# A feed-forward group taken into the mixer projection's stage, its root multiplied in afterwards

## The chip, the cores and the metric

The kernel runs on one core of one Trainium2 chip. The core's engines each run their own queue of instructions: TensorE (PE for its matmuls, PEld for its weight loads), VectorE (DVE), ScalarE (ACT), GpSimd (POOL) and SyncE (SP), which issues the transfers. The metric is the time of one execution on the device in microseconds (us). Times in brackets of a trace row are idle time of that engine just before the row.

## The reference

The network has two blocks; the change lies in the end of the second block, for 256 tokens of 1024 features. With three mixer branches already computed, that end is:

```
mixed = gates[0] * y_ssm + gates[1] * y_rwkv + gates[2] * y_hgrn
x = x + mixed @ w_out
h_gate, h_up = split(rmsnorm(x, norm2_w) @ ffn_w_in, 2)
x = x + (silu(h_gate) * h_up) @ ffn_w_down
return rmsnorm(x, final_norm_w)

def rmsnorm(x, w): return x * rsqrt(mean(x * x, axis=-1) + eps) * w
```

The factor rsqrt(mean(x*x) + eps) is one number for each token; the text calls it the token's root. A product of the normed x with a matrix is the product of x * w with that matrix, times the token's root.

## The kernel before

Activations lie with features on the 128 partitions and tokens along the row, so x is 8 tiles (`h[:, k, CTX:TOK]`, KT = 8) of 128 x 256 in float32. All weights come as one long stream of chunks of 128 x 1024 numbers (512 KB), four chunks to a group here, into `w_ring`, which has two sets of slots. While one set is multiplied the other is filled. SP issues the loads for the next group when the `used` count says that the group before the present one is done (`Stream.in_stage` inside a stage of mixed work, `Stream.groups` for uniform loops). A matmul of 128 x 128 weights with 256 float32 columns shows in the trace as two matmul records.

The program is a row of stages. Each is a block in which every engine has its own instructions, and at the end of a block all engines meet (line 195). Three stages matter:

- `mixer_out` (lines 3360 to 3426). 32 units of output: 8 for each branch (b = 0, 1, 2) and 8 of `w_out` (b = 3). PE sums a unit into one of six PSUM banks. DVE evacuates it; for b = 3 it adds it to x in `h` (L3419). Then the tail of the norm (`NormTail`) follows: ACT squares the new tile (L3205), DVE adds the squares up in `tail_acc` (L3210), PE sums over the partitions (`column_sums`, L155), DVE makes the mean of it (L3224), POOL raises it to the power of -1/2 (L148), PE spreads the roots over the partitions into bank 7 (`spread`, L162), and DVE writes the eight tiles of x * w * root to `u[:, k, CTX:TOK]` (L3231). Six groups of chunks are taken from the stream.
- `swiglu` (lines 3136 to 3175). 11 groups; in each, PE makes four products of 128 x 256 (two gate tiles, two up tiles) out of eight tiles of `u`, that is 32 matmuls (the helper `accumulate`, L410), into four banks, and the groups take banks 0 to 3 and 4 to 7 in turn. ACT takes the tanh of the gate tiles (L3158), DVE makes silu and multiplies by the up tile (L3166, L3169). `walk` runs the first two groups as written, pairs of groups in a loop, and the last ones as written.
- `residual_norm` multiplies by `ffn_w_down`, adds to x and norms again; it follows `swiglu`.

The stage of `swiglu` is entered by PE only when DVE has written the last tile of `u`, since this is the last thing that is done before the engines meet.

Of the kernel before, what the change touches and what calls it, by code (L numbers as in the profile page):

```python
# [17 lines left out]
ALU = mybir.AluOpType  # L18
# [3 lines left out]
P = 128  # L22
# [3 lines left out]
SEQ = 256  # L26
# [2853 lines left out]
def build(nc, a, out, col_at):  # L2880

    with ExitStack() as top:
        used = {}

        def sb(name, shape, es=top):
            used[name] = used.get(name, 0) + 1
            return es.enter_context(nc.sbuf_tensor(f"{name}_{used[name]}", shape, F32))
# [19 lines left out]
        def tail_work(n, es2):  # L2907
            return [sb("tail_" + name, [P] + d, es2) for name, d in (("sq", [2, n]), ("acc", [n]), ("rs", [TT]))]
# [189 lines left out]

        yh = sb("yh", [P, HG, SEQ])
        gates = sb("gates", [P, 24, SEQ])  # L3100
        with ExitStack() as es:
            with ExitStack() as e3:
                work = [sb("hg_" + n, [P] + d, e3) for n, d in (
                    ("e", [2, 512]), ("qx", [2, SEQ]), ("kx", [2, SEQ]), ("sm", [2, SEQ]), ("ib", [2, ST, P]), ("osq", [SEQ]),
                    ("rc", [2, ST]), ("sd", [SEQ]), ("kd", [SEQ]), ("pairs", [LEVELS * P]), ("gt", [HG, SEQ]))]
                hgrn_heads(nc, st, bank, banks, C2, cs, p_hg, lf, kf, cc("hgrn_norm_w"), yh, work, latent, gates[:, 8:24, :], 16, 4)

        with ExitStack() as es:

            mixer_out(nc, st, bank, C, (ys, yr, yh), early, gates, h, hold, late, tail_work(SEQ, es), u, cc("norm2_w"))  # L3110
            nc.sync.sem_clear(late)

        with ExitStack() as es:
            ffn = sb("ffn", [P, FF, SEQ], es)
            ffn_tanh = sb("ffn_tanh", [P, 2, 2, SEQ], es)
            swiglu(nc, st, bank, latent, ffn, ffn_tanh)
# [19 lines left out]
def swiglu(nc, st, bank, src, out, th):  # L3136

    count = FF // 2
    st.begin(4)
    with stage(nc, "used tanh doubled done") as (s, block):  # L3140
        def tensor(pe):
            def visit(g, h, r):
                if not isinstance(g, int) or g >= 2:
                    pe.wait_ge(s["done"], g * 2 - 2)
                for m in range(4):
                    st.wait(pe, h, r, m)
                    mm = accumulate(nc, bank[4 * h + m][:, 0:SEQ], [st.chunk(h, m)[:, P * k:P * k + P] for k in range(KT)],
                                    [src(k) for k in range(KT)])
                mm.then_inc(s["used"], 1)
            walk(pe, count, visit)  # L3150

        def scalar(act):
            def visit(g, h, r):
                act.wait_ge(s["used"], g + 1)
                if not isinstance(g, int) or g >= 2:
                    act.wait_ge(s["done"], g * 2 - 2)
                for m in range(2):
                    nc.scalar.activation(th[:, h, m, :], bank[4 * h + m][:, 0:SEQ], ACT.Tanh, scale=0.5).then_inc(s["tanh"], 1)  # L3158
            walk(act, count, visit)

        def vector(dve):
            def visit(g, h, r):
                for m in range(2):

                    dve.wait_ge(s["tanh"], g * 2 + 2)
                    nc.vector.scalar_tensor_tensor(th[:, h, m, :], th[:, h, m, :], 1.0, bank[4 * h + m][:, 0:SEQ],  # L3166
                                                   ALU.add, ALU.mult).then_inc(s["doubled"], 1)
                    dve.wait_ge(s["doubled"], g * 2 + (m + 1))
                    nc.vector.scalar_tensor_tensor(out[:, bass.ds(g * 2 + m, 1), :].rearrange("p a t -> p (a t)"), th[:, h, m, :], 0.5,  # L3169
                                                   bank[4 * h + 2 + m][:, 0:SEQ], ALU.mult, ALU.mult).then_inc(s["done"], 1)  # L3170
            walk(dve, count, visit)
            dve.wait_ge(s["done"], 2 * count)
# [184 lines left out]
    st.passed(groups, per_body)  # L3357


def mixer_out(nc, st, bank, C, branches, early, gates, h, hold, reloaded, work, u, g_cols):  # L3360
# [8 lines left out]
    with stage(nc, "used mixed " + NormTail.NAMES) as (s, block):  # L3369
# [36 lines left out]
        def _(dve):  # L3406
            link = Chain(dve, s["dve_own"])
            for q, (b, m) in enumerate(units):
                ps, mixed = bank[q % banks][:, 0:SEQ], gates[:, m, :]
# [12 lines left out]
            tail.add(dve, link, KT - 1)  # L3422
            tail.mean(dve, link)
            tail.scale(dve, link, u, g_cols)

    st.passed(6, 4)


def fm(w, cols=None):
# [117 lines left out]
```

## Time and profile before

| what | value |
|---|---|
| median of 3 runs | 2105.58 us (2104.49 to 2110.91) |
| the profiled execution's own time | 2105.29 us |
| its span in the trace | 2103.3 us |
| PE busy in matmuls | 1937.8 us, 92% |
| DVE, ACT, POOL busy | 1019.4, 601.8, 75.3 us |
| mean granted TensorE clock | 0.965 of full |
| stream of weights and other transfers | 184.73 MB, mean 88 GB/s |

A granted clock of 1.00 is 2.4 GHz, 0.50 is 1.2 GHz. The end of a matmul record is modelled; records overlap, so the distance between starts, and not the duration, says how fast they follow each other. The trace's own time runs from the first instruction to the last (the span); the execution takes 1.99 us more.

### The profile page before, as it was taken

What the parts mean: (1) busy time and instruction counts of PE and PEld (TensorE: products, weight loads), DVE (VectorE), ACT (ScalarE), POOL (GpSimd) and SP (SyncE); (2) the same over time, 40 slices, a digit from 0 to 9 for tenths busy, and PEclk for the clock granted to TensorE, in tenths of its full rate; (3) what the DMA queues carried; (4) which work ended last, traced back from release to release, by engine and by line L of the source; (5) the groups of instructions that cost most, each with busy time, mean ns of one, the idle gap of its engine ahead of it and who ended that gap; (6) DMA issues with size and microseconds to landing.
All of it is one profiled execution on the core that took longest, in us unless ns stands there. A gap on an engine that the chain in (4) does not pass through costs nothing. (4 is left out here: it accounts for less than half of the span.)

```text
span 2103.3 us, 40179 instructions
## 1 busy us (share of the span) xinstructions
PE 1937.8 (92%) x16700; PEld 1425.0 (68%) x16700; DVE 1019.4 (48%) x2050; ACT 601.8 (29%) x1287; POOL 75.3 (4%) x51
## 2 busy tenths in 40 slices
PE   6989999999999998798998799989889899989998
PEld 2566666666666766343575687767775898878886
DVE  3456676757676766212125458774545542311001
ACT  2234344434344444201014143233332321000000
POOL 0001010101010110000000000010000000000000
PEclk9999999999999999899999899989999999999999
DMA  9021212111011010222220432231002222433343
GB/s 379 18 82 51 102 41 102 51 62 41 32 32 41 22 41 22 80 80 80 86 80 30 148 136 80 102 112 61 32 33 111 81 80 81 178 112 145 144 180 140
DMA packets 52240, 184.73 MB, mean 88 GB/s; under 512 B 5856, under 2 KB 9312, under 8 KB 51552
## 3 DMA queue, kind: packets, MB, share of 16 engines
q1 hardware_dynamic: 52064, 182.23, 23.7%
q8 instruction: 130, 2.13, 0.4%
q14 instruction: 46, 0.38, 0.1%
HBM read 180.11 MB, written 2.10 MB: 87 GB/s over the span
## 5 line engine op out<-in xcount | busy, mean ns | idle before, releaser
L843 PE MATMUL banks<-u,w_ring 128*128 128x512 f32 x768 | 362.5, 604 | 2.0 <-DVE u L680 2.0
L386 PE MATMUL banks<-u,w_ring 128*128 128x256 f32 x1056 | 251.9, 391 | 8.4 <-PEq L195 8.4
L386 PEld LDWEIGHTS banks<-u,w_ring 128*128 128x128 f32 x1056 | 200.3, 196 | 42.4 <-issue 17.1
L843 PEld LDWEIGHTS banks<-u,w_ring 128*128 128x128 f32 x768 | 139.5, 193 | 124.9 <-issue 117.5
L410 PE MATMUL banks<-u,w_ring 128*128 128x256 f32 x704 | 155.0, 384 | 4.8 <-PEq L195 4.8
L410 PEld LDWEIGHTS banks<-u,w_ring 128*128 128x128 f32 x704 | 135.6, 193 | 24.0 <-issue 5.0
L3316 PE MATMUL banks<-gated,w_ring 128*128 128x512 f32 (+1 forms) x384 | 140.7, 529 | 2.9 <-PEq L195 2.9
L3316 PEld LDWEIGHTS banks<-gated,w_ring 128*128 128x128 f32 x384 | 73.8, 193 | 69.3 <-issue 66.0
L871 DVE SCALAR_TENSOR_TENSOR acc<-raw,hc,acc 128x512 f32<-128x512 f32 x128 | 96.2, 752 | 4.6
L3316 PE MATMUL banks<-ffn,w_ring 128*128 128x256 f32 x352 | 77.9, 385 | 3.0 <-PEq L195 3.0
L3316 PEld LDWEIGHTS banks<-ffn,w_ring 128*128 128x128 f32 x352 | 68.0, 193 | 12.9 <-issue 3.3
L3166 DVE SCALAR_TENSOR_TENSOR ffn_tanh<-ffn_tanh,banks 128x256 f32<-128x256 f32 x22 | 9.2, 418 | 137.9 <-ACT ffn_tanh L3158 137.9
L1269 ACT ACTIVATE acc<-banks 128x512 f32<-128x512 f32 x80 | 47.8, 597 | 83.6 <-PE banks L1092 82.1
L1360 DVE TENSOR_TENSOR acc<-acc,banks 128x512 f32<-128x512 f32 x80 | 55.0, 688 | 32.5 <-PE banks L1108 30.2
L1356 DVE TENSOR_TENSOR y<-banks,const_base 128x512 f32<-128x512 f32 x80 | 55.3, 692 | 28.5 <-PE banks L1080 26.7
L3205 ACT ACTIVATE tail_sq<-h 128x256 f32<-128x256 f32 (+1 forms) x28 | 13.2, 471 | 194.6 <-DVE h L2950 91.7
L1108 PEld LDWEIGHTS banks<-y,acc 64*64 64x64 f32 x2560 | 45.8, 134 | 28.9 <-DVE y L1356 21.8
L1296 ACT ACTIVATE dec<-banks,hs 128x128 f32<-128x128 f32 x128 | 47.0, 367 | 56.9 <-PE banks L1203 53.8
L1381 DVE SCALAR_TENSOR_TENSOR rn<-banks,hs,v_t 128x128 f32<-128x128 f32 x96 | 33.7, 351 | 56.9 <-PE banks L1193 54.3
L1213 PEld LDWEIGHTS banks<-dec,h 128*128 128x128 f32 x256 | 35.7, 197 | 37.1 <-ACT dec L1300 27.1
L1108 PE MATMUL banks<-y,acc 64*64 64x64 f32 x2560 | 55.4, 222 | 3.5 <-DVE y L1356 2.5
L2950 DVE SCALAR_TENSOR_TENSOR h<-banks,mod,h 128x256 f32<-128x256 f32 x16 | 7.7, 484 | 101.8 <-PE banks L3316 101.5
(498 smaller groups left out, 3198.0 us busy)
## 6 DMA issues: line engine op xcount, KB each, us to landing
w_ring<-in_w SPq DMA_DIRECT2D x289, 512.0 KB, 5.6
gated<-in_ada SPq DMA_DIRECT2D x32, 512.0 KB, 4.3
h<-in_h SPq DMA_DIRECT2D x2, 2048.0 KB, 9.6
const_base<-in_const SPq DMA_DIRECT2D x1, 1216.0 KB, 5.3
hold<-h SPq DMA_DIRECT2D x1, 1024.0 KB, 5.2
const_part<-in_const SPq DMA_DIRECT2D x1, 1024.0 KB, 4.7
h<-hold SPq DMA_DIRECT2D x1, 1024.0 KB, 10.2
out<-u SPq DMA_DIRECT2D x8, 128.0 KB, 1.9
```

The source lines that it names most:

```text
L386: mm = self.nc.tensor.matmul(place, self.st.chunk(g % 2, slot)[:, P * k:P * k + P], self.src(k), start=(k == 0), stop=(k == KT - 1))
L410: last = nc.tensor.matmul(out, lhs[k], rhs[k], start=(k == 0), stop=(k == n - 1))
L843: mm = nc.tensor.matmul(self.places[m % len(self.places)][:, :], (st.slot(m) if g is None else st.chunk(g % 2, m))[:, P * k:P * k + P], u[ ...
L871: link(nc.vector.scalar_tensor_tensor(out, raw[:, m, :, i:i + SEQ], hc[:, 5 * m + i:5 * m + i + 1], out, ALU.mult, ALU.add), self.s["conv" ...
L1108: mm = nc.tensor.matmul(block_of(bank[2 * d + j], t, hb), invt_c[half(j), d, 2 * t + hb, :], prod[half(j), d, hb, t, :], start=True, stop= ...
L1213: mm = nc.tensor.matmul(tile(bank[3 + d], j), tile(qkd[:, 2 * j + d, :], t), tile(vn[:, d, :], j), start=True, stop=True)
L1269: link(nc.scalar.activation(invt_c[:, d].rearrange("p s e -> p (s e)"), bank[4 + d][:, :], ACT.Copy), s["t_out"])
L1296: link(nc.scalar.activation(tile(vn[:, d, :], j), tile(bank[2], 2 * d + j), ACT.Copy, scale=col(BETA, 2 * j + d, t)), s["vn_ready"] if j a ...
L1356: link(nc.vector.tensor_tensor(prod[:, d], both(sums(2 * d, 256)), mask(d, lv), ALU.mult), s["p_ready"])
L1360: link(nc.vector.tensor_tensor(by_chain(inv[:, d]), by_chain(inv[:, d]), both(sums(2 * d, 256)), ALU.subtract), s["t_ready"])
L1381: link(nc.vector.scalar_tensor_tensor(tile(resid[:, d, :], j), tile(bank[0], 2 * d + j), col(NEG_EG, 2 * j + d, t), v_t[:, t, j, :], ALU.m ...
L3316: mm = nc.tensor.matmul(bank[m % banks][:, 0:n], st.chunk(g % 2, c)[:, P * (at % 8):P * (at % 8) + P], src(k), start=(k == 0), stop=(k == ...
```

## The change

The first of the 11 feed-forward groups moves from `swiglu` into the end of `mixer_out`, which now takes seven groups from the stream. It is summed from x * w without the root. For this ACT writes x * w to the free half of `u` (`u[:, k, 0:SEQ]`) as soon as a tile of x is there, ahead of its square. PE does the group's four products (`rough`) around the tail's own two steps. The units' banks are turned by four places, so that the products can go to banks 0 to 3. ACT copies the spread roots from bank 7 to a new tile `root` in SBUF, and DVE's eight scaling instructions read them there. In `swiglu` DVE first multiplies the four banks by `root` and goes on with silu; ten groups are left for the loop, and they start with the other half of the banks.

```diff
 def swiglu(nc, st, bank, src, out, th, root):
-    count = FF // 2
+    count = FF // 2 - 1
...
-                if not isinstance(g, int) or g >= 2:
-                    pe.wait_ge(s["done"], g * 2 - 2)
+                if not isinstance(g, int) or g >= 1:
+                    pe.wait_ge(s["done"], g * 2)
...
-                    mm = accumulate(nc, bank[4 * h + m][:, 0:SEQ], [st.chunk(h, m)[:, P * k:P * k + P] for k in range(KT)],
+                    mm = accumulate(nc, bank[4 - 4 * h + m][:, 0:SEQ], [st.chunk(h, m)[:, P * k:P * k + P] for k in range(KT)],
...
         def scalar(act):
+            for m in range(2):
+                act.wait_ge(s["rooted"], 2 * m + 2)
+                nc.scalar.activation(out[:, m, :], th[:, 0, m, :], ACT.Tanh, scale=0.5).then_inc(s["rough_tanh"], 1)
...
         def vector(dve):
+            for m in range(2):
+                for up in range(2):
+                    nc.vector.tensor_tensor(th[:, up, m, :], bank[2 * up + m][:, 0:SEQ], root, ALU.mult).then_inc(s["rooted"], 1)
+            for m in range(2):
+                dve.wait_ge(s["rooted"], 2 * m + 2)
+                dve.wait_ge(s["rough_tanh"], m + 1)
+                nc.vector.scalar_tensor_tensor(out[:, m, :], out[:, m, :], 1.0, th[:, 0, m, :], ALU.add, ALU.mult).then_inc(s["doubled"], 1)
+                dve.wait_ge(s["doubled"], m + 1)
+                nc.vector.scalar_tensor_tensor(out[:, m, :], out[:, m, :], 0.5, th[:, 1, m, :], ALU.mult, ALU.mult).then_inc(s["done"], 1)
...
-    through = [0, 4, 8, 16, 24, 28, 32]
+    place = lambda q: (q + 4) % banks
+    through = [0, 4, 8, 16, 24, 28, 32, 33]
...
-        st.in_stage(6, 4, s["used"], block, through, {3: reload})
+        st.in_stage(7, 4, s["used"], block, through, {3: reload})
...
-                    mm = nc.tensor.matmul(bank[q % banks][:, 0:SEQ], st.chunk(g % 2, c)[:, P * at:P * at + P],
+                    mm = nc.tensor.matmul(bank[place(q)][:, 0:SEQ], st.chunk(g % 2, c)[:, P * at:P * at + P],
...
-            tail.sums(pe)
+            def rough(c):
+                st.wait(pe, 6 % 2, 6 // 2, c)
+                pe.wait_ge(s["evacuated"], len(units) - banks + c + 1)
+                for k in range(KT):
+                    if c == 0:
+                        pe.wait_ge(s["primed"], k + 1)
+                    mm = nc.tensor.matmul(bank[c][:, 0:SEQ], st.chunk(6 % 2, c)[:, P * k:P * k + P], u[:, k, 0:SEQ],
+                                          start=(k == 0), stop=(k == KT - 1))
+                return mm
+            rough(0)
+            pe.wait_ge(s["added"], KT - 1)
+            column_sums(nc, C, bank[7], tail.acc, tail.tiles).then_inc(s["sums"], 1)
+            rough(1)
+            pe.wait_ge(s["root"], 1)
+            spread(nc, C, bank[7], tail.rs, tail.tiles).then_inc(s["spread"], 1)
+            rough(2)
+            rough(3).then_inc(s["used"], 1)
...
             for k in range(KT):
+                act.wait_ge(s["evacuated"], 3 * KT + k + 1)
+                link(nc.scalar.activation(u[:, k, 0:SEQ], tail.tile(k), ACT.Copy, scale=g_cols[:, k:k + 1]), s["primed"])
                 tail.square(act, link, k)
+            act.wait_ge(s["spread"], 1)
+            link(nc.scalar.activation(root, bank[7][:, 0:SEQ], ACT.Copy), s["copied"])
...
             tail.mean(dve, link)
-            tail.scale(dve, link, u, g_cols)
+            dve.wait_ge(s["copied"], 1)
+            tail.scale(dve, link, u, g_cols, root)
```

On PE, at the end of `mixer_out`, the program reads as follows; L3394 is the units' matmul of before and L3409 the same line after, L3420 is the matmul of `rough`, L155 the column sums, L162 the spread, L195 the meeting of the engines. Counts are matmuls.

```order
-L3394 MATMUL banks<-gates,w_ring 128x256 x64
+L3396 UNCONDITIONAL_BRANCH
+L3409 MATMUL banks<-u,w_ring 128x256 x64
+L3409 MATMUL banks<-yr,w_ring 128x256 x32
+L3409 MATMUL banks<-yh,w_ring 128x256 x32
+L3409 MATMUL banks<-gates,w_ring 128x256 x64
+L3420 MATMUL banks<-u,w_ring 128x256 x8
 L155 MATMUL banks<-const_base,tail_acc 128x1 x2
+L3420 MATMUL banks<-u,w_ring 128x256 x8
 L162 MATMUL banks<-const_base,tail_rs 128x128 x2
+L3420 MATMUL banks<-u,w_ring 128x256 x16
 L195 UNCONDITIONAL_BRANCH
```

Before, the column sums came straight behind the units and the spread straight behind the sums; now 8 matmuls stand ahead of each of the two and 16 behind the spread.

On ACT, at the end of `mixer_out` and the start of `swiglu`; L3205 is the square of before and L3219 the same after, L3438 writes x * w, L3441 copies the roots, L3156 is the tanh of the moved group and L3158 (after: L3162) that of the others.

```order
+L3438 ACTIVATE u<-h,cols 128x256
+L3219 ACTIVATE tail_sq<-h 128x256
+L3441 ACTIVATE root<-banks 128x256
 L195 UNCONDITIONAL_BRANCH
 L288 UNCONDITIONAL_BRANCH
-L3158 ACTIVATE ffn_tanh<-banks 128x256 x4
+L3156 ACTIVATE ffn<-ffn_tanh 128x256 x2
+L3162 ACTIVATE ffn_tanh<-banks 128x256 x4
```

Each of the eight squares now has one more instruction of ACT ahead of it, and one copy stands behind the last square.

On SP, around the reload of a spilled tile inside `mixer_out` (L3374 before, L3389 after); L215 is the load of one chunk, L304 the clearing of the ring's counts ahead of the stage's last group of loads.

```order
 L215 DMA w_ring<-in_w 128x1024 x16
-L3374 DMA h<-hold 128x8x256
-L215 DMA w_ring<-in_w 128x1024 x4
+L3389 DMA h<-hold 128x8x256
+L215 DMA w_ring<-in_w 128x1024 x8
 L304 ISA
 L215 DMA w_ring<-in_w 128x1024 x4
```

Four chunk loads have moved from the stage of `swiglu` into this one, behind the reload.

## Rows read from the trace of the kernel before

**Rows 1.** The page, its parts 1 and 5: busy time by engine; costliest groups by line.

```profile
PE 1937.8 (92%) x16700; PEld 1425.0 (68%) x16700; DVE 1019.4 (48%) x2050; ACT 601.8 (29%) x1287; POOL 75.3 (4%) x51
...
L410 PE MATMUL banks<-u,w_ring 128*128 128x256 f32 x704 | 155.0, 384 | 4.8 <-PEq L195 4.8
```

**Rows 2.** The timeline of the mixer projection's end: start us, duration us, engine, line.

```profile
1844.80 2.75 PE L3394 MATMUL banks<-gates,w_ring 128*128 128x256 f32 x12
...
1847.66 0.42 DVE L3419 SCALAR_TENSOR_TENSOR h<-banks,h 128x256 f32<-128x256 f32 x1 [2.57 <-PE banks L3394]
1848.12 0.99 DVE L3210 TENSOR_TENSOR tail_acc<-tail_acc,tail_sq 128x256 f32<-128x256 f32 x2
1848.17 0.42 ACT L3205 ACTIVATE tail_sq<-h 128x256 f32<-128x256 f32 x1 [3.04 <-DVE h L3419]
...
1849.17 0.61 PE L155 MATMUL banks<-const_base,tail_acc 128*128 128x1 f32 x4 [1.61 <-DVE tail_acc L3210]
1849.88 0.16 DVE L3224 TENSOR_SCALAR tail_rs<-banks 128x2 f32<-128x2 f32 x1 [0.77 <-PE banks L155]
1850.12 0.69 POOL L148 TENSOR_TENSOR tail_rs<-tail_rs,const_base 128x2 f32<-128x2 f32 x1 [89.79 <-DVE tail_rs L3224]
...
1850.87 0.43 PE L162 MATMUL banks<-const_base,tail_rs 128*128 128x128 f32 x2 [1.10 <-POOL tail_rs L148]
1851.42 4.10 DVE L3231 SCALAR_TENSOR_TENSOR u<-h,cols,banks 128x256 f32<-128x256 f32 x8 [1.38 <-PE banks L162]
...
1856.11 24.18 PE L410 MATMUL banks<-u,w_ring 128*128 128x256 f32 x98 [4.81 <-PEq L195]
1856.21 18.53 SPq L215 DMA_DIRECT2D w_ring<-in_w  x8
1872.99 0.66 ACT L3158 ACTIVATE ffn_tanh<-banks 128x256 f32<-128x256 f32 x2 [24.41 <-PE banks L410]
```

**Rows 3.** Busy time and granted clock of PE by stretches: start:end, length, busy, PEclk.

```profile
1848.00:1851.00 3.00, 0.73 (x5) 1.00 0.00 0
1851.50:1856.00 4.50, 0.00 (x0) 0.50 0.00 0
1857.00:1861.00 4.00, 4.00 (x11) 0.50 0.79 294
1862.50:1866.50 4.00, 4.00 (x20) 1.00 0.25 100
1900.00:1950.00 50.00, 50.00 (x233) 1.00 0.45 168
1462.00:1465.00 3.00, 1.85 (x31) 1.00 0.00 0
...
2015.50:2018.50 3.00, 3.00 (x9) 0.50 0.90 345
```

**Rows 4.** The timeline of ACT in the feed-forward groups, second and last.

```profile
1886.81 0.66 ACT L3158 ACTIVATE ffn_tanh<-banks 128x256 f32<-128x256 f32 x2 [13.16 <-PE banks L410]
...
2011.13 0.66 ACT L3158 ACTIVATE ffn_tanh<-banks 128x256 f32<-128x256 f32 x2 [13.07 <-PE banks L410]
```

**Rows 5.** The timeline of PE at 1089 us, a spread that waits for nothing.

```profile
1089.15 0.60 PE L162 MATMUL banks<-const_base,att_rq 128*128 128x128 f32 x4
1089.59 3.60 PE L1518 MATMUL banks<-kf,pqz 128*128 128x512 f32 x8
```

**Rows 6.** The boundary between two stages at 1370 us, by line L195.

```profile
L195 PEldq EVENT_SEMAPHORE  x2: 51/51/51, 1369.3 to 1370.1; - x2
...
L195 ACTq EVENT_SEMAPHORE  x2: 17/17/17, 1369.9 to 1370.1; - x2
```

**Rows 7.** The timeline of PE at 1370 us, behind that boundary.

```profile
1370.18 1.10 PE L386 MATMUL banks<-u,w_ring 128*128 128x256 f32 x4 [0.99 <-PEq L195]
```

**Rows 8.** The timeline of PE at 1464 us, behind another boundary.

```profile
1463.90 1.97 PE L2235 MATMUL banks<-const_part,lw_rw 128*128 128x256 f32 x8 [1.15 <-PEq L195]
```

**Rows 9.** The timeline of PE behind the feed-forward groups.

```profile
2014.05 6.24 PE L3316 MATMUL banks<-ffn,w_ring 128*128 128x256 f32 x20 [2.96 <-PEq L195]
```

**Rows 10.** DMA from 1825 to 1880 us in 40 slices of 1.375 us.

```profile
DMA  9400000898930000000000059688100000039898
GB/s 366 197 6 0 0 0 0 259 405 313 399 149 0 12 0 0 0 0 0 0 0 0 0 176 393 244 304 331 77 0 0 0 0 0 0 92 381 331 355 331
```

**Rows 11.** What the DMA queue itself waited for, 1760 to 2103 us.

```profile
SPq L215 <- PE banks L410: 107.5, 9, 15.0
```

More of the change, by code:

```diff
@@ L3100, in build @@
         gates = sb("gates", [P, 24, SEQ])
+        root = sb("root", [P, SEQ])
         with ExitStack() as es:
@@ L3108, in build @@
         with ExitStack() as es:
-            mixer_out(nc, st, bank, C, (ys, yr, yh), early, gates, h, hold, late, tail_work(SEQ, es), u, cc("norm2_w"))
+            mixer_out(nc, st, bank, C, (ys, yr, yh), early, gates, h, hold, late, tail_work(SEQ, es), u, cc("norm2_w"), root[:, :])
             nc.sync.sem_clear(late)
@@ L3115, in build @@
             ffn_tanh = sb("ffn_tanh", [P, 2, 2, SEQ], es)
-            swiglu(nc, st, bank, latent, ffn, ffn_tanh)
+            swiglu(nc, st, bank, latent, ffn, ffn_tanh, root[:, :])
             def add(m, ps, link, done):
@@ L3133, in build, with swiglu @@
         st.drain()
-def swiglu(nc, st, bank, src, out, th):
-    count = FF // 2
+def swiglu(nc, st, bank, src, out, th, root):
+    count = FF // 2 - 1
     st.begin(4)
-    with stage(nc, "used tanh doubled done") as (s, block):
+    with stage(nc, "rooted rough_tanh used tanh doubled done") as (s, block):
         def tensor(pe):
             def visit(g, h, r):
-                if not isinstance(g, int) or g >= 2:
-                    pe.wait_ge(s["done"], g * 2 - 2)
+                if not isinstance(g, int) or g >= 1:
+                    pe.wait_ge(s["done"], g * 2)
                 for m in range(4):
                     st.wait(pe, h, r, m)
-                    mm = accumulate(nc, bank[4 * h + m][:, 0:SEQ], [st.chunk(h, m)[:, P * k:P * k + P] for k in range(KT)],
+                    mm = accumulate(nc, bank[4 - 4 * h + m][:, 0:SEQ], [st.chunk(h, m)[:, P * k:P * k + P] for k in range(KT)],
                                     [src(k) for k in range(KT)])
@@ L3152, in scalar @@
         def scalar(act):
+            for m in range(2):
+                act.wait_ge(s["rooted"], 2 * m + 2)
+                nc.scalar.activation(out[:, m, :], th[:, 0, m, :], ACT.Tanh, scale=0.5).then_inc(s["rough_tanh"], 1)
             def visit(g, h, r):
                 act.wait_ge(s["used"], g + 1)
-                if not isinstance(g, int) or g >= 2:
-                    act.wait_ge(s["done"], g * 2 - 2)
+                act.wait_ge(s["done"], max(g * 2, 2) if isinstance(g, int) else g * 2)
                 for m in range(2):
-                    nc.scalar.activation(th[:, h, m, :], bank[4 * h + m][:, 0:SEQ], ACT.Tanh, scale=0.5).then_inc(s["tanh"], 1)
+                    nc.scalar.activation(th[:, 1 - h, m, :], bank[4 - 4 * h + m][:, 0:SEQ], ACT.Tanh, scale=0.5).then_inc(s["tanh"], 1)
             walk(act, count, visit)
         def vector(dve):
+            for m in range(2):
[7 more added lines that the diff above has]
+                nc.vector.scalar_tensor_tensor(out[:, m, :], out[:, m, :], 0.5, th[:, 1, m, :], ALU.mult, ALU.mult).then_inc(s["done"], 1)
             def visit(g, h, r):
@@ L3165, in visit @@
                     dve.wait_ge(s["tanh"], g * 2 + 2)
-                    nc.vector.scalar_tensor_tensor(th[:, h, m, :], th[:, h, m, :], 1.0, bank[4 * h + m][:, 0:SEQ],
+                    nc.vector.scalar_tensor_tensor(th[:, 1 - h, m, :], th[:, 1 - h, m, :], 1.0, bank[4 - 4 * h + m][:, 0:SEQ],
                                                    ALU.add, ALU.mult).then_inc(s["doubled"], 1)
-                    dve.wait_ge(s["doubled"], g * 2 + (m + 1))
-                    nc.vector.scalar_tensor_tensor(out[:, bass.ds(g * 2 + m, 1), :].rearrange("p a t -> p (a t)"), th[:, h, m, :], 0.5,
-                                                   bank[4 * h + 2 + m][:, 0:SEQ], ALU.mult, ALU.mult).then_inc(s["done"], 1)
+                    dve.wait_ge(s["doubled"], g * 2 + (m + 3))
+                    nc.vector.scalar_tensor_tensor(out[:, bass.ds(g * 2 + (2 + m), 1), :].rearrange("p a t -> p (a t)"), th[:, 1 - h, m, :],
+                                                   0.5, bank[6 - 4 * h + m][:, 0:SEQ], ALU.mult, ALU.mult).then_inc(s["done"], 1)
             walk(dve, count, visit)
-            dve.wait_ge(s["done"], 2 * count)
+            dve.wait_ge(s["done"], 2 * count + 2)
         st.groups(count, 4, s, block, ((block.tensor, tensor), (block.scalar, scalar), (block.vector, vector)))
@@ L3357, in residual_norm, with mixer_out @@
     st.passed(groups, per_body)
-def mixer_out(nc, st, bank, C, branches, early, gates, h, hold, reloaded, work, u, g_cols):
+def mixer_out(nc, st, bank, C, branches, early, gates, h, hold, reloaded, work, u, g_cols, root):
     banks = 6
     units = [(b, m) for b in range(4) for m in range(KT)]
-    through = [0, 4, 8, 16, 24, 28, 32]
+    place = lambda q: (q + 4) % banks
+    through = [0, 4, 8, 16, 24, 28, 32, 33]
     st.begin(4)
-    with stage(nc, "used mixed " + NormTail.NAMES) as (s, block):
+    with stage(nc, "used mixed primed copied " + NormTail.NAMES) as (s, block):
         tail = NormTail(nc, C, s, bank[7], h, CTX, SEQ, work, 3 * KT)
@@ L3408, in _ @@
             for q, (b, m) in enumerate(units):
-                ps, mixed = bank[q % banks][:, 0:SEQ], gates[:, m, :]
+                ps, mixed = bank[place(q)][:, 0:SEQ], gates[:, m, :]
                 own = gates[:, 8 * b + m, :] if b < 3 else None
@@ L3423, in _ @@
             tail.mean(dve, link)
-            tail.scale(dve, link, u, g_cols)
-    st.passed(6, 4)
+            dve.wait_ge(s["copied"], 1)
+            tail.scale(dve, link, u, g_cols, root)
+    st.passed(7, 4)
 def fm(w, cols=None):
```

## The prediction, made before the changed kernel ran

> **What bounds the kernel now.** I read the page first: PE is busy for 92% of the span, every other engine for less than half [rows 1]. So what counts is where PE stands still or runs slowly near the change, and the next view is the timeline of the place where one stage hands over to the other [rows 2]. The reader is to follow one chain there. The last record of the mixer's matmuls ends at 1844.80 + 2.75 = 1847.55. DVE then takes the tile (1847.66), ACT squares it (1848.17), DVE adds, PE sums at 1849.17, DVE and POOL make the root (done at 1850.81), PE spreads it from 1850.87, and DVE writes eight scaled tiles from 1851.42, for 4.10 us. Only then can the engines meet, and the first feed-forward matmul starts at 1856.11. From 1847.55 to there are 8.56 us, in which PE's own work is 0.61 + 0.43 us.
>
> The granted clock, read next by stretches [rows 3], shows a second loss. It is 1.00 (2.4 GHz) when PE falls silent, 0.50 (1.2 GHz) from 1851.5 on, still 0.50 between 1857 and 1861 with PE busy throughout, and 1.00 from 1862.5. So group 0 of the feed-forward runs its first records at half speed.
>
> What that costs comes from ACT, whose tanh marks the end of each group. Groups 1 and 10 end at 1886.81 and 2011.13 [rows 4], nine groups apart: 124.32 / 9 = 13.81 us a group. A group is 704 / 11 = 64 records [rows 1], so 0.216 us each, in agreement with 233 records in 50 us at full clock, some records being lost [rows 3]. Group 0 took 1872.99 - 1856.11 = 16.88 us [rows 2]. At full clock it would take 13.81 plus about 0.3 us (the first weight load uncovered, the last record running out, ACT's start), my estimate from the same rows: a record lasts longer than the 0.216 between starts. So 14.1 us, and 2.8 us are lost to the clock.
>
> **The change part by part.** All times are against the profiled execution.
>
> PE, what goes. The idle stretch of 8.56 us is filled by a group that had to be done anyway: -8.56. The group now follows the units without a pause, and its start at half clock goes: -2.8.
>
> PE, what stays as work. Column sums and spread now stand between products. The trace has a spread that waits for nothing, between long matmuls: four records take 1089.59 - 1089.15 = 0.44 us, 0.11 each [rows 5]. Here it is four records for the sums and two for the spread [rows 2]: 6 x 0.11 = 0.66. The upper bound is their stand-alone time, 0.61 + 0.43 = 1.04. I take +0.66, since they are ready when PE comes to them, as in rows 5. The products and these end at 1847.55 + 13.81 + 0.66 = 1862.0.
>
> PE, the new boundary. Before, PE waited there for DVE; now PE is last. At 1370 us PE reached the meeting at 1369.3 and ACT at 1369.9, and PE's pause was 0.99 us [rows 6, 7]; another boundary has 1.15 [rows 8]. In both a slower engine came after PE. In the first, 0.3 us pass from the last arrival to PE's next matmul, and PE and SP need some 0.15 to arrive. So the bounds are 0.45 and 1.15, and I take +0.6, near the lower one because nothing is expected behind PE. Group 1 then starts at 1862.6 and ends at 1876.7, against 1886.81.
>
> What must be ready for PE, with its slack. (a) Product 0, step 7 needs the last x * w. DVE's tile is there at 1848.08, ACT's new instruction, 0.42 like the square beside it [rows 2], ends at about 1848.6, and PE asks at 1847.55 + 7 x 0.43 = 1850.6: slack 2. (b) The squares are now behind that instruction: last square to 1849.1, last add (0.5) to 1849.6, PE asks for the sums at 1847.55 + 3.45 = 1851.0: slack 1.4. (c) Sums done at 1851.4; the root came 1.03 us after them before (1849.78 to 1850.81), so at 1852.5, and PE wants it at 1854.9: slack 2.4. (d) ACT copies the roots at about 1855.2 (two tanh from PSUM take 0.66, so 0.33), DVE scales for 4.1 us to 1859.8, and its arrival at the meeting has 2.2 us in hand. Reading the roots from SBUF has no row of its own; the instruction that reads a bank beside SBUF takes 0.42 at L3419 and 0.51 here [rows 2], so 3.4 to 4.1 in all, and both fit. Each of these costs nothing while its slack holds, and one for one beyond it.
>
> The stream. The moved group's chunks were already loaded in this stage: the DMA share falls to zero after slice 11 from 1834.6, that is by 1841.5 [rows 10], 6 us before `rough` asks. The next group is now issued when the units end, at 1847.6, instead of at 1856.21 [rows 2]; the same load took until about 1864.9 then (slices 23 to 28), 9 us, so it lands at about 1856 for a use at 1862.6. The reload of the tile sits ahead of both in SP's queue as before. SP waited for PE 107.5 us in nine waits in the feed-forward loop, not PE for SP [rows 11].
>
> DVE and ACT in `swiglu`. The moved group is finished behind PE's group 1: four multiplications, two tanh, four steps of silu, ten instructions of at most 0.5 us, some 4 us with their waits, from 1862.5. PE asks for those banks only at the next group, at 1876.7, and ACT has nothing else till then. The waits of the later groups keep their distance of two groups.
>
> Sum: -8.56 - 2.8 + 0.66 + 0.6 = -10.1 us. All later stages only move up. 2105.29 - 10.1 = 2095.2 in the profiled execution; the median of before lies 0.29 above it, so 2095.5.
>
> **The rivals.**
>
> *The clock still falls.* PE's stream is now interrupted three times within 15 us: sums, spread, boundary. If one of them lets the clock fall as it did at 1851.5, PE runs at half speed for the length of that fall, some 10 us [rows 3], and loses 5: gain 5.1, time 2100.4. For it: the pause of 2.96 us behind the feed-forward [rows 9] is followed by a stretch at 0.50 [rows 3]. Against: around the 1.15 us pause of rows 8 the clock stays 1.00 [rows 3], and each interruption here is shorter.
>
> The Trainium skill ("TensorE: Matmul & The Clock Gate", section "A second HAM failure mode: psum-queue depth-cycling") speaks for this rival: short idle gaps between groups of matmuls, as they move from bank to bank, were seen to make the clock swing and to cost throughput. By that rule the time would be the 2100.4 just given; the feed-forward loop of this trace, which changes banks all the time at 1.00, does not bear it out, and I leave it little.
>
> *The tail chain is late.* If one of (a) to (d) is over its slack, PE stands there. What is wanted for a loss is more than 1.4 us of unseen latency in a chain of 2 us; the price is then 1 or 2 us, 2096.5 to 2097.5. It stays inside my range.
>
> *The stream is the bound.* Then PE's head start is given back as a wait for chunks before the next groups, and the time is 2105.5. Against it: PE is busy 50.00 of 50.00 us in the loop while the DMA share is 0.45 [rows 3], and up to 405 GB/s against 168 were moved [rows 10].
>
> *Slower.* The low clock stays: from the sums on PE is never again busy enough, and works at 1.2 GHz until the feed-forward loop is well under way. Half clock costs half of its length, so it breaks even at 20 us and shows as slower beyond 33 us. If it lasted from 1851 to the end of group 2, 42 us, it would cost 21 and give 2116.5. In this trace half clock ended some 6 us after PE was busy again [rows 2, 3], which is strongly against it.
>
> *The change doesn't do what it says.* The order on PE shows 32 matmuls ahead of the boundary and 32 fewer behind, so only unexpected waits could undo it.
>
> **How the numbers follow.** Forecast 0.80; late tail 0.04; clock falls 0.10; stream 0.03; slower 0.03. The likeliest is 2095.5. One fall of the clock behind the pause of rows 9 costs about 1.5 us (3 us at half [rows 3]) and may come or not in a given run, and the boundary adds 0.15 or takes 0.55. That gives 2093.3 to 2098; towards the rival at 2100.4 I go on to 2101, and 2092.8 below. A difference under 0.3%, 6.3 us, is not told from none. Forecast, a short fall of the clock and late tail are faster: 0.85. The full fall and the stream are within 0.3%: 0.12. Slower: 0.03.
>
> **What would show it.** In the profile after: L3420 starts within 0.3 us of the end of the units; sums and spread in 0.11 us a record with no pause before either; PEclk 1.00 from 1848 to past 1865; a pause of PE of 0.5 to 1.2 us at the boundary, DVE there first by about 2 us; the tanh of the first group that `swiglu` sums at about 1876.7, the other nine 13.81 us apart, and the end of the last ten us earlier. The forecast is wrong if PE pauses before L155 or L162, if a stretch at 0.50 lies in the first group of `swiglu`, or if the loop's groups become longer.

## The result, and the profile after

The changed kernel is faster: 2092.18 us median of 5 runs (2091.18 to 2094.99), against 2105.46 us (2101.63 to 2110.91) of the kernel before, a ratio of 0.9937 (95% interval 0.9919 to 0.9955), that is 13.3 us. The forecast was 2095.5 us in a range from 2092.8 to 2101.0. Direction and mechanism were right; the time lies 0.6 us below the range. In two further sets of runs (e2 and e8 below) the ratio was 0.9949 and 0.9948, 10.7 and 10.9 us.

The place of the change, in the timeline of the kernel after (start us, duration us, engine, line; L3409 is the units' matmul, L3420 the moved group's, L3457 the evacuation, L3438 x * w, L3219 the square):

```profile
1839.80 4.48 PE L3409 MATMUL banks<-gates,w_ring 128*128 128x256 f32 x20
...
1844.11 3.62 PE L3420 MATMUL banks<-u,w_ring 128*128 128x256 f32 x16
...
1844.38 0.42 DVE L3457 SCALAR_TENSOR_TENSOR h<-banks,h 128x256 f32<-128x256 f32 x1 [2.57 <-PE banks L3409]
...
1844.90 0.51 ACT L3438 ACTIVATE u<-h,cols 128x256 f32<-128x256 f32 x1 [2.50 <-DVE h L3457]
...
1845.96 0.42 DVE L3224 TENSOR_TENSOR tail_acc<-tail_acc,tail_sq 128x256 f32<-128x256 f32 x1 [0.70 <-ACT tail_sq L3219]
...
1847.57 0.50 PE L155 MATMUL banks<-const_base,tail_acc 128*128 128x1 f32 x4
...
1848.41 0.69 POOL L148 TENSOR_TENSOR tail_rs<-tail_rs,const_base 128x2 f32<-128x2 f32 x1 [91.08 <-DVE tail_rs L3238]
...
1851.46 0.38 PE L162 MATMUL banks<-const_base,tail_rs 128*128 128x128 f32 x2
...
1851.94 0.38 ACT L3441 ACTIVATE root<-banks 128x256 f32<-128x256 f32 x1 [6.08 <-PE banks L162]
1852.47 4.13 DVE L3245 SCALAR_TENSOR_TENSOR u<-h,cols,root 128x256 f32<-128x256 f32 x8 [4.13 <-ACT root L3441]
...
1859.21 23.12 PE L410 MATMUL banks<-u,w_ring 128*128 128x256 f32 x106 [0.45 <-PEq L195]
...
1873.30 0.66 ACT L3162 ACTIVATE ffn_tanh<-banks 128x256 f32<-128x256 f32 x2 [12.22 <-PE banks L410]
```

Against [rows 2] the reader is to see four things. The first `rough` matmul starts at 1844.11, before the modelled end of the units' last record (1839.80 + 4.48 = 1844.28). The column sums (L155) and the spread (L162) have no idle time before them. DVE scales from 1852.47 to 1856.60, while PE works to 1858.75, so the last eight instructions that [rows 2] had in front of the feed-forward cost nothing. And the pause of PE at the boundary is 0.45 us instead of 4.81. The granted clock of the same stretches (length, busy, PEclk):

```profile
1844.00:1848.00 4.00, 4.00 (x23) 1.00 0.64 236
1848.00:1852.00 4.00, 4.00 (x21) 1.00 0.74 289
1852.00:1859.00 7.00, 6.75 (x32) 1.00 0.00 0
1859.00:1863.00 4.00, 3.79 (x18) 1.00 0.69 244
...
2002.00:2005.00 3.00, 3.00 (x9) 0.50 0.96 335
```

It is 1.00 from the units through the whole first group of `swiglu`, where [rows 3] had 0.50 from 1851.5 to past 1861. The stretch at 0.50 behind the feed-forward loop is still there. ACT's second and last tanh of the loop's ten groups:

```profile
1887.11 0.66 ACT L3162 ACTIVATE ffn_tanh<-banks 128x256 f32<-128x256 f32 x2 [13.16 <-PE banks L410]
...
1997.62 0.66 ACT L3162 ACTIVATE ffn_tanh<-banks 128x256 f32<-128x256 f32 x2 [13.15 <-PE banks L410]
```

(1997.62 - 1887.11) / 8 = 13.81 us a group, as in [rows 4].

Where the whole difference lies is told by four stretches: all stages ahead of the mixer projection, that stage, `swiglu`, and what follows. First before, then after (start:end, length, busy, PEclk):

```profile
0.00:1762.72 1762.72, 1618.04 (x15249) 0.97 0.21 76
1762.72:1856.11 93.39, 85.87 (x390) 0.96 0.40 147
1856.11:2014.05 157.94, 154.98 (x704) 0.98 0.39 146
2014.05:2103.30 89.25, 78.94 (x358) 0.95 0.44 165
```

```profile
0.00:1759.47 1759.47, 1612.70 (x15248) 0.97 0.21 76
1759.47:1859.21 99.74, 99.29 (x455) 0.98 0.42 158
1859.21:2000.54 141.33, 138.37 (x640) 1.00 0.40 149
2000.54:2089.40 88.86, 78.94 (x358) 0.95 0.44 166
```

From the first matmul of the mixer projection to the first one behind the loop it is 2014.05 - 1762.72 = 251.33 us before and 2000.54 - 1759.47 = 241.07 after: 10.26 less. Behind that, 0.39 less. But the first stretch, with the same program, is shorter too: 3.25. Together 13.9 of span, and 0.2 outside it (about 2.0 us of the execution lie outside the span before, 1.8 after). The profiled execution of the changed kernel, 2091.18 us, is also the fastest of its five. The text below calls the 251.33 and 241.07 the *distance*.

### The profile page after: what moved, and what is told of

It is laid out like the page before. It is cut to its first block and busy times, and to the rows that moved or that the text cites. A ratio compares the mean times of both kernels' runs of the same rounds, so it can differ in the third digit from the quotient of the medians.

```text
span 2089.4 us, 40176 instructions
## 1 busy us (share of the span) xinstructions
PE 1929.3 (92%) x16700; PEld 1418.8 (68%) x16700; DVE 1020.4 (49%) x2054; ACT 606.4 (29%) x1296; POOL 75.3 (4%) x51
## 5 line engine op out<-in xcount | busy, mean ns | idle before, releaser
L386 PE MATMUL banks<-u,w_ring 128*128 128x256 f32 x1056 | 249.7, 388 | 8.4 <-PEq L195 8.4
L386 PEld LDWEIGHTS banks<-u,w_ring 128*128 128x128 f32 x1056 | 198.8, 194 | 41.7 <-issue 17.1
L843 PEld LDWEIGHTS banks<-u,w_ring 128*128 128x128 f32 x768 | 139.5, 193 | 125.0 <-issue 117.7
L410 PE MATMUL banks<-u,w_ring 128*128 128x256 f32 x640 | 138.4, 379 | 0.5 <-PEq L195 0.5
L410 PEld LDWEIGHTS banks<-u,w_ring 128*128 128x128 f32 x640 | 121.5, 190 | 17.3 <-issue 0.8
L3219 ACT ACTIVATE tail_sq<-h 128x256 f32<-128x256 f32 (+1 forms) x28 | 13.2, 470 | 173.5 <-DVE h L2950 91.7
```

Source lines behind the costliest of these rows:

```text
L386: mm = self.nc.tensor.matmul(place, self.st.chunk(g % 2, slot)[:, P * k:P * k + P], self.src(k), start=(k == 0), stop=(k == KT - 1))
L410: last = nc.tensor.matmul(out, lhs[k], rhs[k], start=(k == 0), stop=(k == n - 1))
L843: mm = nc.tensor.matmul(self.places[m % len(self.places)][:, :], (st.slot(m) if g is None else st.chunk(g % 2, m))[:, P * k:P * k + P], u[ ...
```

## The experiments

Ten runs. Each measured gain comes from the ratio to the kernel before, timed beside it; a 95% interval stands behind it. The changed kernel's own gain by distance is 10.25 us, and a variant's profile says how much of that it keeps. The table gives, for each profile, where the mixer projection starts, the distance, and the length from there to the end.

| kernel | start of mixer projection | distance | to the end | ratio (95%) |
|---|---|---|---|---|
| before | 1762.72 | 251.33 | 89.22 | |
| after | 1759.47 | 241.07 | 88.82 | 0.9937 (0.9919 to 0.9955) |
| e1 before again | 1761.28 | 251.34 | 89.21 | 1.0000 (0.9991 to 1.0009) |
| e2 after again | 1761.00 | 241.10 | 88.83 | 0.9949 (0.9936 to 0.9963) |
| e8 after, third time | 1763.62 | 241.07 | 88.82 | 0.9948 (0.9934 to 0.9962) |
| e7 places only | 1766.87 | 251.34 | 89.22 | 0.9999 (0.9990 to 1.0009) |
| e3 keep busy | 1763.55 | 248.54 | 89.22 | 0.9989 (0.9979 to 0.9999) |
| e4 root first | 1760.77 | 246.42 | 88.52 | 0.9966 (0.9954 to 0.9978) |
| e5 root last | 1764.12 | 248.89 | 88.83 | 0.9992 (0.9982 to 1.0002) |
| e9 spread late | 1764.32 | 244.23 | 87.15 | 0.9972 (0.9961 to 0.9983) |
| e6 early tanh, on after | 1769.48 | 239.47 | 87.14 | 0.9928 (0.9914 to 0.9941) |
| e10 early tanh alone | 1761.28 | 249.73 | 87.14 | 0.9979 (0.9970 to 0.9988) |

### e1, e2, e7, e8: are the 3 us ahead of the change its own?

Two theories. A: they are scatter of the unchanged stages, and the change is worth 10.6. B: the change's layout (a new tile, turned banks, other addresses) makes the stages ahead faster.

e1 is the kernel before with no edit.

> The kernel before, unchanged, once more. In the profiles the way from the start of the mixer projection to the end of the feed-forward loop became 10.3 us shorter, but the stages ahead of it, which the change does not touch, were 3.2 us shorter too. Theory A (chance): those 3.2 us are where the granted clock happened to fall; this run's mixer projection starts anywhere between 1758 and 1765 us of its span, and its median lies within 2 us of the other runs of before. Theory B (the change moves something upstream): it starts at 1762.7 within 0.5 us, as in the first profile, and the times of before stay 13 us above those of the changed kernel.

e2 is the changed kernel with no edit.

> The changed kernel, unchanged, once more. Theory A: its gain over the kernel before on this chip is 10 us, within 2, when more rounds are taken, and its mixer projection starts anywhere between 1757 and 1763 us. Theory B: the gain is 13 us again and the mixer projection starts at 1759.5 within 0.5 us. Both: local distance from the first mixer matmul to the first matmul behind the feed-forward loop 241.1 us, against 251.3 before.

e7 is the kernel before with this edit:

```diff
+    place = lambda q: (q + 4) % banks
-  mm = nc.tensor.matmul(bank[q % banks][:, 0:SEQ], ...
+  mm = nc.tensor.matmul(bank[place(q)][:, 0:SEQ], ...
-  ps, mixed = bank[q % banks][:, 0:SEQ], gates[:, m, :]
+  ps, mixed = bank[place(q)][:, 0:SEQ], gates[:, m, :]
+  root = sb("root", [P, SEQ])
```

(shortened; `ps, mixed` is the line of DVE's evacuation, and the tile `root` stays unused)

> The kernel before with only the units' banks turned by four places and the unused tile root laid out. Theory A (nothing upstream is moved by the change's layout; a first profile with 3 us less there was chance): no difference, median within 2 us of before, distance 251.3. Theory B (layout): faster by 2 to 3 us, with a mixer projection that starts 3 us earlier.

e8 is the changed kernel with no edit.

> The changed kernel a third time. Theory A: gain 10.6 us (10.2 between the first mixer matmul and the first one behind the loop, 0.4 behind it), within 2; start of the mixer projection between 1757 and 1764. Theory B: gain 13.

Measured: in e1 the median was 2104.35 (the kernel before, timed beside it: 2104.94), in e7 2105.34 (2105.11), in e2 2093.78 (2104.94), in e8 2094.66 (2105.11). The distance repeats to 0.03 us, in three profiles with the changed group (after, e2, e8) and in three without (before, e1, e7). The start of the mixer projection does not: 1762.72 and 1761.28 for before, 1759.47, 1761.00 and 1763.62 for after, and 1766.87 for e7, though all run the same program up to there. The second profile of the changed kernel, first two stretches:

```profile
0.00:1761.00 1761.00, 1615.02 (x15249) 0.97 0.21 76
1761.00:1860.76 99.76, 99.31 (x454) 0.98 0.43 158
```

1761.00 stands against 1761.28 of e1: only 0.3 is left of the 3.25. B has fallen: neither does e7's layout alone gain anything, nor does the changed kernel start the stage early each time. A holds. What makes the scatter is not settled in full, but much of it goes with the clock. Added up from the clock records of the twelve profiles, the time at half clock ahead of the mixer projection runs from 112.6 us (e10, which reaches it at 1761.28) to 143.4 (e6, at 1769.48), with 122.8 in before and 116.1 in the first one of after; its correlation with the start is 0.89. The 6.7 us less at half in the first one of after are worth up to 3.4 us, about the 3.25 in question. It is not the whole: e1 has before's 122.8 and is there 1.4 us sooner. Why the clock falls for longer in one execution than in the next is not shown. Likewise, of the eleven runs of e7 the two slowest (2109.44 and 2109.90) have a mean granted clock of 0.961 and the fastest (2101.40) one of 0.968. e1's expectation was that the start lies between 1758 and 1765; e7's lay outside even of that.

The gain of the change is then the distance, 10.25, and 0.4 behind it: 10.65. The 0.2 us outside the span belong to it too, since they repeat: 1.77 to 1.80 us lie outside the span in all seven profiles of the changed kernel and its variants, and 1.96 to 2.07 in the five of the kernel before and its variants. That makes about 10.9. The three measured gains, 13.3, 10.7 and 10.9 with intervals of 3 to 4 us to either side, all hold it.

### e3: what the clock alone is worth

The kernel before, with matmuls whose result nobody reads, in the idle stretch:

```diff
-            tail.sums(pe)
+            def filler(n):
+                for k in range(n):
+                    nc.tensor.matmul(bank[3][:, 0:SEQ], st.chunk(5 % 2, 3)[:, P * k:P * k + P], gates[:, k, :], start=(k == 0), stop=(k == n - 1))
+            pe.wait_ge(s["evacuated"], 28)
+            filler(3)
+            pe.wait_ge(s["added"], KT - 1)
+            column_sums(...)
+            filler(2)
+            pe.wait_ge(s["root"], 1)
+            spread(...)
+            filler(8)
```

> The kernel before, with 13 matmuls whose result nobody reads put into the idle stretch of the mixer projection's end (3 ahead of the column sums, 2 ahead of the spread, 8 behind it), so that PE is nearly never idle there but nothing is done earlier. Theory 1 (the 2.8 us of group 0 were the clock's, as in the forecast): the clock stays at 1.00 and the gain is 2.8 us, local distance 248.5. Rival (the clock falls anyway at sums, spread or boundary, and the changed kernel owes its speed to work alone): a stretch at 0.50 in group 0, gain 0 to 1.

Timeline of PE in e3, and the clock (L3400 is the filler):

```profile
1848.22 1.46 PE L3400 MATMUL banks<-gates,w_ring 128*128 128x256 f32 x6
1850.00 0.61 PE L155 MATMUL banks<-const_base,tail_acc 128*128 128x1 f32 x4 [0.32 <-DVE tail_acc L3210]
1850.47 1.11 PE L3400 MATMUL banks<-gates,w_ring 128*128 128x256 f32 x4
1851.70 0.43 PE L162 MATMUL banks<-const_base,tail_rs 128*128 128x128 f32 x2
1851.97 3.62 PE L3400 MATMUL banks<-gates,w_ring 128*128 128x256 f32 x16
1856.94 5.42 PE L410 MATMUL banks<-u,w_ring 128*128 128x256 f32 x24 [1.35 <-PEq L195]
```

```profile
1852.00:1856.00 4.00, 3.59 (x18) 1.00 0.00 0
1856.00:1860.00 4.00, 3.06 (x14) 1.00 0.45 168
```

The pause at the boundary is 1.35 us, the start of `swiglu` is where it was, 93.39 us behind the start of the mixer projection in both, and the clock is 1.00. The distance became 248.54: 2.79 less, with no useful work done earlier. The measured gain, 2.3 us (0.2 to 4.4), agrees, though alone it would leave room for the rival's 0 to 1; the profile decides. So the term of the sum for the clock, 2.8, is shown by itself, and the rival fell.

### e4: both of the root's steps ahead of the products

```diff
-            rough(0)
             pe.wait_ge(s["added"], KT - 1)
             column_sums(...)
-            rough(1)
             pe.wait_ge(s["root"], 1)
             spread(...)
-            rough(2)
-            rough(3).then_inc(s["used"], 1)
+            rough(0), rough(1), rough(2), rough(3).then_inc(s["used"], 1)
```

> The changed kernel with the column sums and the spread ahead of all four products of the moved group, so that PE waits for them. Theory 1: PE waits 2.1 us for the sums and 1.1 us for the root with the clock still at 1.00, so 3.2 us slower than the changed kernel, 7 us faster than before. Rival (those two short waits already make the clock fall, as the whole tail did before): 5 us more, 8 slower than the changed kernel, about 2 faster than before.

Timeline of PE and clock in e4:

```profile
1847.77 0.61 PE L155 MATMUL banks<-const_base,tail_acc 128*128 128x1 f32 x4 [2.17 <-DVE tail_acc L3224]
1849.47 0.62 PE L162 MATMUL banks<-const_base,tail_rs 128*128 128x128 f32 x2 [1.10 <-POOL tail_rs L148]
1849.89 15.51 PE L3420 MATMUL banks<-u,w_ring 128*128 128x256 f32 x64
1865.86 4.34 PE L410 MATMUL banks<-u,w_ring 128*128 128x256 f32 x19 [0.45 <-PEq L195]
```

```profile
1848.00:1850.00 2.00, 0.90 (x7) 0.89 0.91 350
1850.00:1852.00 2.00, 2.00 (x6) 0.50 0.97 342
1852.00:1854.00 2.00, 2.00 (x8) 0.75 0.38 154
```

PE waits 2.17 and 1.10 us, as foreseen, and the clock falls to 0.50, but for less time than behind the whole tail of before: the three means (0.89, 0.50, 0.75 over 2 us each) add up to 3.4 us at half, a loss of 1.7. The distance is 5.35 us above the changed kernel's: 3.3 for the waits, 1.7 for the clock, and 0.4 for the two steps, which now stand alone (0.61 us and, to the next start, 0.42, for 0.66 together). Neither expectation had it; it lies between the two. The measured gain over before, 7.2 us (4.6 to 9.7), cannot tell whether the clock falls in every execution: 5.8 by this profile and 7.5 without the fall both fit. What interleaving the products brings is these 5.3 us, more than the waits themselves.

### e5: both behind the products

The changed kernel's lines once more in another order: `rough(0)` to `rough(3)` first, then the wait for the sums, the sums, the wait for the root and the spread.

> The changed kernel with all four products of the moved group ahead of the column sums and the spread, so that the root chain and DVE's eight scalings are uncovered again. Theory 1 (the gain is the cover of that chain): PE idles as before, sums at 14 us behind the units, then 1.1 us for the root, 0.9 for spread and copy, 4.1 for DVE and 0.3 for the boundary: 7 us more than the changed kernel, and the clock falls for the first group of the loop, 2.8 more. Local distance 251, about the time of before. Rival (what gained is that the group left the loop): stays within 2 us of the changed kernel, distance 243.

```profile
1862.61 0.50 PE L155 MATMUL banks<-const_base,tail_acc 128*128 128x1 f32 x4
1864.21 0.43 PE L162 MATMUL banks<-const_base,tail_rs 128*128 128x128 f32 x2 [1.10 <-POOL tail_rs L148]
1869.98 10.35 PE L410 MATMUL banks<-u,w_ring 128*128 128x256 f32 x39 [5.34 <-PEq L195]
```

```profile
1870.50:1873.00 2.50, 2.50 (x7) 0.50 0.78 247
```

The root's chain lies bare again: 0 for the sums, 1.10 for the root, 5.34 us at the boundary, and the clock is at 0.50 behind it. The distance is 248.89, 7.8 more than the changed kernel's and not 9.8; the clock took back 1.7 us, not 2.8, since it rose again after eight records and not thirteen. So theory 1 is right in kind and 2 us too high in size. Of the 7.8, 4.9 are the boundary (5.34 less 0.45), 1.1 the root and 1.7 the clock. Three quarters of the distance gained are gone (measured gain over before: 1.7 us, -0.4 to 3.8), although the group has left the loop here as well. The gain is in covering the root's chain and DVE's scalings, not in the move alone.

### e9: the spread one product later

```diff
             rough(1)
+            rough(2)
             pe.wait_ge(s["root"], 1)
             spread(...)
-            rough(2)
             rough(3).then_inc(s["used"], 1)
```

> The changed kernel with the spread one product later (behind product 2 instead of product 1). In the changed kernel DVE came to the meeting 2.0 us ahead of PE. Theory 1 (a slack costs nothing until it is used up, then one for one): the spread comes 3.45 us later, so PE now waits 3.45 - 2.0 = 1.5 us for DVE, distance from the first mixer matmul to the first one behind the loop 242.6 instead of 241.1, clock still 1.00 behind the boundary. Rival (the pause of about 2 us at the boundary makes the clock fall): 1.7 to 2.8 us more, distance 244 to 245.5.

```profile
1859.80 0.38 PE L162 MATMUL banks<-const_base,tail_rs 128*128 128x128 f32 x2
1860.02 3.62 PE L3420 MATMUL banks<-u,w_ring 128*128 128x256 f32 x16
1865.53 10.77 PE L410 MATMUL banks<-u,w_ring 128*128 128x256 f32 x41 [1.89 <-PEq L195]
```

```profile
1866.00:1868.00 2.00, 2.00 (x8) 0.70 0.62 195
1868.00:1869.50 1.50, 1.50 (x5) 0.50 1.02 410
...
1870.00:1873.00 3.00, 3.00 (x15) 0.96 0.73 298
```

PE's pause is 1.89 instead of 0.45 us: 1.44 more, where 3.45 less a slack of 2.0 had given 1.5. So the slack (d) is real and goes one for one. But the clock falls too behind this pause, for 3.4 us (from 1866.8 to 1870.2 by the shares above), and the distance grew by 3.16: 1.44 and 1.7. Both theories had a part; the rival's lower end was right on the clock. The measured gain, 5.9 us (3.6 to 8.2), sides with the fall: without it some 9.4 would be due (10.9 less 1.44), with it 7.7. The profile's own 9.2 (7.1 of distance, 2.1 behind it) holds a piece of luck shown next.

### e6 and e10: the end of the loop

In each group of the loop, PE signals when the gate products are done. The core of the edit (e6 on the changed kernel, e10 the same on the kernel before; `(1 + tanh) * gate` and `0.5 * that * up` stand for DVE's two instructions):

```diff
+                    if m == 1:
+                        mm.then_inc(s["gate"], 1)
                 mm.then_inc(s["used"], 1)
...
-                act.wait_ge(s["used"], g + 1)
+                act.wait_ge(s["gate"], g + 1)
...
+                dve.wait_ge(s["tanh"], g * 2 + 2)
                 for m in range(2):
-                    dve.wait_ge(s["tanh"], g * 2 + 2)
                     (1 + tanh) * gate
+                dve.wait_ge(s["used"], g + 1)
+                for m in range(2):
                     0.5 * that * up
```

> The changed kernel, in whose feed-forward groups PE signals already when the two gate products are done; ACT takes tanh and DVE its first step beside the two up products, so that behind a group's last matmul only two DVE instructions are left. It should take 1.5 us out of the pause of 2.96 us behind the last group (to 1.4) and, if the clock then no longer falls behind it, up to 1.7 us more. Distance from the mixer projection's first matmul to the first one behind the loop 239.6; gain over before 12 to 14. Rival (DVE's steps beside PE's last products slow them, or ACT's earlier tanh makes PE wait for banks): distance 241 or more.

> The kernel before with only the earlier signal of the gate products in the feed-forward loop. If its gain is independent of the moved group, it is the 1.6 us of distance and the 1.7 us behind the loop that it gave on top of the changed kernel: distance 249.7, 87.5 us from there to the end, 3.3 us faster than before. Rival (it is worth something only with the shifted loop, or the clock falls behind the loop anyway): distance 249.7, but 89.2 to the end, 1.6 us faster.

Timeline of e6 at the end of the loop (L3164 tanh, L3181 DVE's first step, L3186 its last):

```profile
2000.71 0.66 ACT L3164 ACTIVATE ffn_tanh<-banks 128x256 f32<-128x256 f32 x2 [13.16 <-PE banks L410]
2001.40 0.75 DVE L3181 SCALAR_TENSOR_TENSOR ffn_tanh<-ffn_tanh,banks 128x256 f32<-128x256 f32 x2 [6.84 <-ACT ffn_tanh L3164]
2007.62 0.75 DVE L3186 SCALAR_TENSOR_TENSOR ffn<-ffn_tanh,banks 128x256 f32<-128x256 f32 x2 [5.46 <-PE banks L410]
...
2008.94 1.32 PE L3333 MATMUL banks<-ffn,w_ring 128*128 128x256 f32 x5 [1.36 <-PEq L195]
```

The pause is 1.36 instead of 2.96 us [rows 9], and the distance 239.47 and 249.73: 1.6 less on top of either kernel. Behind it 87.14 us follow in both, 1.7 less than after and 2.1 less than before, with no fall of the clock there. For e10 87.5 had been expected; the missing 0.4 is the early start of DVE's scaling that "Why the prediction came out as it did" tells of. Measured: 15.2 us for e6 (12.4 to 18.1; 12 to 14 expected), the fastest kernel of this study at 2091.18 us, beside 2094.66 for the changed kernel; 4.4 us (2.5 to 6.3) for e10. The 1.6 us are shown. That the missing fall of the clock comes from the shorter pause is likely only. The clock fell behind the loop in nine of the ten profiles with the pause at its full length and in neither of the two with 1.36 us, but in the tenth, that of e9, it did not fall either:

```profile
2008.55 7.79 PE L3330 MATMUL banks<-ffn,w_ring 128*128 128x256 f32 x35 [2.96 <-PEq L195]
```

```profile
2010.00:2012.00 2.00, 2.00 (x11) 1.00 1.00 389
```

## Why the prediction came out as it did

**What bounds the kernel; idle 8.56 us, clock 2.8 us.** Right: the mechanism was the one forecast. From the end of the units to the tanh of the second group it was 1886.81 - 1847.55 = 39.26 us [rows 2, 4]. After, it is 1873.30 - 1844.28 = 29.02 to the same group's tanh. The forecast was 29.15 (1876.7 - 1847.55). The clock's part stands alone in e3: 2.79.

**Sums and spread, +0.66; boundary, +0.6.** From the end of the units to the first matmul of `swiglu`: 1859.21 - 1844.28 = 14.93 us, predicted 15.07 (13.81 + 0.66 + 0.6). The six short records took what was worked out from [rows 5], and the pause was 0.45, the lower bound; I had taken 0.15 more.

**The slacks.** All held: no wait before L155 or L162. ACT's new instruction takes 0.51, not the 0.42 of the square; the last add runs to 1845.96 + 0.42 = 1846.38, 1.2 us ahead of the sums (predicted 1.4). Reading the roots from SBUF made DVE's eight scalings no shorter: 4.13 us, at the upper bound of the 3.4 to 4.1 taken. DVE was 2.0 us ahead of PE at the meeting (1856.90 to 1858.87 in the trace's semaphore events; predicted 2.2), and e9 used it up one for one.

**The stream, DVE and ACT in `swiglu`.** As predicted: no wait for chunks, groups of 13.81 us.

**The sum's starting point, "all later stages only move up", and the range.** This step failed. The sum subtracts the place's 10.1 us from one execution of before (2105.29) and puts nothing, without a reason, for all that lies outside the place. In the profiled executions 4.0 us lie between forecast and result (2095.2 and 2091.18): 3.25 in the stages ahead of the mixer projection, 0.39 behind the loop, 0.2 outside the span and 0.16 at the place itself (10.26 for 10.1). The last three, 0.75 together, are the change's own and were missed; with them the forecast would have been 2094.7, inside the range. What put the result outside it was scatter, and by luck it went the way of the gain: the unchanged stages ahead differ by up to 10 us between profiles of the same program (1759.47 to 1769.48 in the table), and the medians of the changed kernel by up to 2.5 (2092.18, 2093.78, 2094.66), of which the first is the lowest and the later two lie inside the range.

The range left no room for this. Its terms were the boundary (adds 0.15 or takes 0.55) and one fall of the clock (1.5); about 2095.5 they give 2093.9 to 2097.6, not the 2093.3 to 2098 put down, and 2092.8 has no term of its own. A low end near 2090.5 would have been honest: the three times of before that I had (2104.49, 2105.58, 2110.91) already spread over 6 us.

**Behind the loop, -0.39, and outside the span, -0.2.** Not foreseen. In the last stage DVE's first scaling starts 0.4 us sooner after the spread (1.38 instead of 1.77 us idle), in all eight profiles of kernels whose DVE program was edited ahead of it, e10 among them, and in none of the four (before, e1, e3, e7) where it has the same instructions as before. The instruction itself was not edited. What makes it wait stays open, and so does what lies in the 0.2 us outside the span.

**The rivals.** That the clock still falls did not happen here but is no idle fear: it fell in e4 after 2.17 + 1.10 us of pauses, and in e9 behind one of 1.89. Its price was 1.7 us (3.4 us at half) in each, not the 5 that I had put on it. The late tail, the stream as the bound and the lasting low clock were not seen.

The rule that I had weighed from the Trainium skill ("TensorE: Matmul & The Clock Gate", section "A second HAM failure mode: psum-queue depth-cycling") did not show: with the products running from bank to bank the clock was 1.00 from 1844 to 1863 in the profile after. That short pauses can cost more than their length is borne out by e4 and e9 all the same.

## What to carry to other kernels

Where a norm's scale is one number per column of the product, start the next product from the unscaled data and multiply the scale in at evacuation; place the reduction and the spread between the products, as early as their inputs allow, so that the chain behind them is covered too (7.8 us hung on that order here, e5, out of 10.3). Price an idle stretch of TensorE with the slow records behind it: 8.6 us idle cost 2.8 more, and a filler whose result nobody reads got these back (e3). Put the scatter of the whole program into the range, not only the bounds of the edited terms, and read a gain off the distance between two events around the edit, which repeated to 0.03 us where the total moved by several.

## What the runs showed of the hardware that was not expected

- The granted clock fell behind a single pause of PE of 1.89 us (one profile, e9) and not behind pauses of 1.35 us (e3), 1.15 us [rows 3, 8] or 0.45 us (after). Behind the same pause of 2.96 us it fell in nine of ten profiles. So what a pause of 2 to 3 us costs in this kernel is a risk of 1.7 us, not a fixed price.
- Short pauses close together are another case. Ahead of the mixer projection PE pauses for 0.98, 1.17 and 1.65 us with only the small products of a sum and a spread between them, and the first 3.58 us of the stage run at a mean granted clock of 0.52, before the change as after it (0.52 over 3.53 us).
- When TensorE was the last to arrive at the end of a block, its pause was 0.45 us (after, e4); in [rows 7, 8] it was 0.99 and 1.15 with another engine last.
- ACT's copy with a scale per partition took 0.51 us for 128 x 256 from SBUF (L3438), its square 0.42 (L3219), and its copy of the roots from a PSUM bank without such a scale 0.38 (L3441).
